# Modulation chunks loaded and summed one merge sooner, and the last norm by column halves, in a two-block float32 model on one core

## The reference, cut to what matters

```python
# first block, for each of the two layers
mod = silu(c) @ ada_w[l] + ada_b[l]                 # 1024 x 3072
shift, scale, gate = split(mod, 3)
h = rms_norm(x, pre_norm[l]) * (1 + scale) + shift
p = split_proj(h @ w_in[l])      # ret, dsa, gla parts and "merge", 3 x 1024 columns
ret, dsa, gl = retention(..), dsa_attention(..), gla(..)   # each normed or gated by silu
g = sigmoid(p["merge"])
y = g0 * (ret @ w_br_ret) + g1 * (dsa @ w_br_dsa) + g2 * (gl @ w_br_gla)
x = x + gate * rms_norm(y @ w_out[l], post_norm[l])
# second block: an even layer (windowed attention and a gated MLP) and an odd one
# (latent attention), with x = x + gate * y, and at the end
out = rms_norm_2(x, final_g)     # x * rsqrt(mean(x*x) + 1e-6) * final_g
```

## Time and profile before

| | us |
|---|---|
| median of three runs | 1077.6 (1077.05 to 1078.86) |
| the profiled execution, its own time | 1079.21 |
| its span | 1077.4 |
| TensorE busy (PE) | 1042.0 |
| TensorE weight loads (PEld) | 757.8 |
| VectorE busy (DVE) | 601.1 |
| ScalarE busy (ACT) | 477.9 |
| GpSimd busy (POOL) | 76.6 |

### The profile page before, as it was taken

One profiled execution on the slowest core, in us unless ns is written; L12 is line 12 of the kernel. 1 busy time (PEld: TensorE's weight loads), 2 busy tenths in 40 slices (PEclk: granted clock), 3 DMA queues, 4 the chain that ended last, 5 costly groups with the idle time before them and its releaser, 6 DMA issues.

```text
span 1077.4 us, 13519 instructions
## 1 busy us (share of the span) xinstructions
PE 1042.0 (97%) x5208; PEld 757.8 (70%) x5208; DVE 601.1 (56%) x1177; ACT 477.9 (44%) x942; POOL 76.6 (7%) x103
## 2 busy tenths in 40 slices
PE   7999999999999999999999999999999999999997
PEld 5688875777467888857874587777677888556553
DVE  2429966595655299754454744236745555245742
ACT  3437547462134365476540353246535423225641
POOL 3001110000000020110000000500000001230000
PEclk9999999999999999999999999999999999999999
DMA  9645432476624355335467362422642015242000
GB/s 385 277 164 203 182 134 101 156 293 276 251 90 170 140 208 203 113 130 219 189 243 304 121 234 79 156 98 79 235 157 103 1 40 220 112 156 98 2 1 39
DMA packets 13743, 171.29 MB, mean 159 GB/s; under 512 B 1504, under 2 KB 1760, under 8 KB 3056
## 3 DMA queue, kind: packets, MB, share of 16 engines
q1 hardware_dynamic: 13216, 168.82, 41.0%
q10 hardware_dynamic: 464, 1.61, 0.4%
HBM read 169.37 MB, written 1.05 MB: 158 GB/s over the span
## 4 chain that ended last, share of the span: by engine, by line
PE 83%; DVE 7%; ACT 6%; DMA 2%; issue 1%; SPq 0%; DVEq 0%; ACTq 0%
PE bank L786 15%; PE bank L1132 8%; PE bank L1081 8%; PE bank L1021 7%; PE bank L1179 6%; PE bank L756 5%; PE bank L1138 5%; PE bank L1114 4%; PE bank L1316 3%; PE bank L764 3%; PE bank L866 3%; PE bank L1393 2%; PE bank L719 2%; PE bank L1381 1%; PE bank L727 1%
## 5 line engine op out<-in xcount | busy, mean ns | idle before, releaser
L1505 ACT ACTIVATE whi<-ring 128x512 fp32r<-128x512 f32 x120 | 73.6, 631 | 65.3 <-PE bank L786 65.3
L2169 DVE TENSOR_TENSOR wlo<-ring,whi 128x512 fp32r<-128x512 f32 x120 | 82.2, 708 | 32.8 <-ACT whi L1505 32.5
L786 PE MATMUL bank<-whi,xhi 128*128 128x512 f32 (+1 forms) x256 | 98.2, 384 | 1.3 <-ACT dsag L1428 1.3
L786 PE MATMUL bank<-wlo,xhi 128*128 128x512 f32 (+1 forms) x256 | 96.4, 377 | 0.0
L786 PE MATMUL bank<-whi,xlo 128*128 128x512 f32 (+1 forms) x256 | 96.4, 376 | 0.0
L764 PE MATMUL bank<-ring,hT 128*128 128x512 f32 (+1 forms) x160 | 61.2, 536 | 0.2 <-ACT hT L1448 0.2
L1138 PE MATMUL bank<-ring,hT 128*128 128x256 f32 (+2 forms) x224 | 57.9, 418 | 3.3 <-ACT hT L1471 2.3
L1021 PE MATMUL bank<-merge_high,xhi 128*128 128x512 f32 x144 | 58.2, 404 | 1.6 <-ACT retqkv L1428 1.1
L1021 PE MATMUL bank<-ring_low,xhi 128*128 128x512 f32 x144 | 56.9, 395 | 0.0
L1021 PE MATMUL bank<-merge_high,xlo 128*128 128x512 f32 x144 | 56.9, 395 | 0.0
L786 PEld LDWEIGHTS bank<-whi,xhi 128*128 128x128 f32 x256 | 48.2, 188 | 11.8 <-ACT dsag L1428 1.6
(11 more groups left out here) (414 smaller groups left out, 2198.3 us busy)
## 6 DMA issues: line engine op xcount, KB each, us to landing
ring<-in_weights SPq DMA_DIRECT2D x73, 2048.0 KB, 8.1
ring<-in_weights SPq DMA_DIRECT2D x5, 1024.0 KB, 5.0
ring<-in_weights SPq DMA_DIRECT2D x2, 1360.0 KB, 10.3
ring<-in_weights SPq DMA_DIRECT2D x1, 1536.0 KB, 8.3
kk<-in_k SPq DMA_DIRECT2D x1, 1120.0 KB, 7.7
X<-in_x SPq DMA_DIRECT2D x1, 1024.0 KB, 14.6
kc<-in_k ACTq DMA_DIRECT2D x1, 1024.0 KB, 10.6
X<-in_context SPq DMA_DIRECT2D x1, 1024.0 KB, 10.1
```

The costliest lines, as they stand in the source:

```text
L786: mm = pe.matmul(o[:, 0:width], a, b[:, q % BUFFERS, at], start=(k == 0 and m == 0), stop=(k == KD - 1 and m == 2))
L1505: act.activation(whi1[:, q % BUFFERS, :], w, ACT.Copy).then_inc(event("hi1_ready"), 1)
L2169: dve.tensor_tensor(wlo1[:, q % BUFFERS, :], piece1(q)[2], whi1[:, q % BUFFERS, :], ALU.subtract).then_inc(event("lo1_ready"), 1)
```

## The change

1. RING1: the chunks ada0 to ada5 are loaded one place sooner, each ahead of merge m + 1, all through slot 0; the merges take slots 2 and 1 in turn.
2. Chunk 0 is summed in g = 6 (layer 0, on VectorE, ahead of gla_take(6)) or behind gla_g (layer 1, on TensorE, in bank 1); chunk m in merge m (VectorE) or behind merge m - 1 (TensorE). Its columns come behind merge m, up to chunk 4; chunk 5's stay where they were. The banks of the sums and columns are new.
3. The last norm goes by column halves: the square, the addition and the product with the gain by halves of 512 columns, the scaling of the low half on VectorE and of the high half on ScalarE, and four stores instead of two.

```diff
-         ("dsa_g", KD * 512, 0), ("gla_g", KD * 512, 1), ("merge0", KD * 512, 2), ("merge1", KD * 512, 0),
-         ("ada0", KD * 512, 1), ("merge2", KD * 512, 2), ("ada1", KD * 512, 1), ("merge3", KD * 512, 0),
-         ("ada2", KD * 512, 1), ("merge4", KD * 512, 2), ("ada3", KD * 512, 1), ("merge5", KD * 512, 0),
-         ("ada4", KD * 512, 1), ("br0", 4 * D, 2), ("ada5", KD * 512, 1), ("br1", 4 * D, 0), ("br2", 4 * D, 1),
+         ("dsa_g", KD * 512, 0), ("gla_g", KD * 512, 1), ("merge0", KD * 512, 2), ("ada0", KD * 512, 0),
+         ("merge1", KD * 512, 1), ("ada1", KD * 512, 0), ("merge2", KD * 512, 2), ("ada2", KD * 512, 0),
+         ("merge3", KD * 512, 1), ("ada3", KD * 512, 0), ("merge4", KD * 512, 2), ("ada4", KD * 512, 0),
+         ("merge5", KD * 512, 1), ("ada5", KD * 512, 0), ("br0", 4 * D, 2), ("br1", 4 * D, 0), ("br2", 4 * D, 1),
...
+        if name == "gla_g1" and summed_on_pe(l, 0):
+            u.append(("s_ada0", 1))
         if name.startswith("merge") and name.endswith("1"):
             m = int(name[5])
-            if summed_on_pe(l, m):
-                u.append((f"s_ada{m}", 0 if m else 1))
-            if m:
-                u.append((f"ada{m - 1}", 1))
+            if summed_on_pe(l, m + 1):
+                u.append((f"s_ada{m + 1}", (0, 0, 4)[m]))
+            if m < MERGES - 1:
+                u.append((f"ada{m}", (1, 1, 5, 2, 1)[m]))
...
+                    if name == "gla_g" and summed_on_pe(l, 0):
+                        ada_rows(u, "ada0", landed("ada0"))
                     if name.startswith("merge"):
                         m = int(name[5])
-                        if summed_on_pe(l, m):
-                            ada_rows(u, f"ada{m}", landed(f"ada{m}"))
-                        if m > 0:
-                            ada1(l, m - 1)
+                        if summed_on_pe(l, m + 1):
+                            ada_rows(u, f"ada{m + 1}", landed(f"ada{m + 1}"))
+                        if m < MERGES - 1:
+                            ada1(l, m)
...
-                    if name.startswith("merge") and summed_on_pe(l, int(name[5])):
-                        m = int(name[5])
+                    if name == "gla_g" and summed_on_pe(l, 0):
+                        ada_out(u, "ada0", msum[0])
+                    if name.startswith("merge") and summed_on_pe(l, int(name[5]) + 1):
+                        m = int(name[5]) + 1
                         ada_out(u, f"ada{m}", msum[m % 2], f"ada{m - 2}" if m > 1 else None)
...
                         if name[0:5] == "merge" and t == 0 and int(name[5]) > 0:
-                            chunk_sum(int(name[5]) - 1)
+                            chunk_sum(int(name[5]))
                         gla_sub(g + 2)
                         gla_mul(g + 1)
+                        if g == 6:
+                            chunk_sum(0)
...
-                        if m == MERGES - 1:
-                            chunk_sum(m)
-                        if m > 0:
-                            own = m - 1 >= SHIFTS
-                            mod_out(u, f"ada{m - 1}", m - 1, l if own else l + 1, conds(l, m - 1))
+                        if m < MERGES - 1:
+                            own = m >= SHIFTS
+                            mod_out(u, f"ada{m}", m, l if own else l + 1, conds(l, m))
...
             for t in range(TT):
-                act.wait_ge(event("x3_ready"), t + 1)
-                act.activation(Y2[:, TT + t, :], X[:, t, :], ACT.Square, accum_out=st2[:, t:t + 1]).then_inc(event("f_ssq"), 1)
-                act.wait_ge(event("f_var"), t + 1)
-                act.activation(st2[:, 8 + t:9 + t], st2[:, 4 + t:5 + t], ACT.Sqrt).then_inc(event("f_std"), 1)
+                for h in range(2):
+                    act.wait_ge(event("x3_ready"), 2 * t + h + 1)
+                    act.activation(Y2[:, TT + t, h * 512:(h + 1) * 512], X[:, t, h * 512:(h + 1) * 512], ACT.Square,
+                                   accum_out=st2[:, 2 * t + h:2 * t + h + 1]).then_inc(event("f_ssq"), 1)
+                act.wait_ge(event("f_part"), t + 1)
+                act.wait_ge(event("f_ssq"), 2 * t + 2)
+                act.activation(st2[:, 8 + t:9 + t], st2[:, 2 * t + 1:2 * t + 2], ACT.Sqrt, scale=1.0 / D,
+                               bias=st2[:, 4 + t:5 + t]).then_inc(event("f_std"), 1)
+                act.wait_ge(event("f_scale"), t + 1)
+                act.activation(Y2[:, t, 512:1024], Y2[:, t, 512:1024], ACT.Copy,
+                               scale=st2[:, 28 + t:29 + t]).then_inc(event("high_out"), 1)
...
+            dve.wait_ge(event("fing_in"), 16)
             for t in range(TT):
-                step(add_half(u, "oout", t, 0, 0, Y2[:, t, 0:512]))
-                add_half(u, "oout", t, 1, 0, Y2[:, t, 512:1024]).then_inc(event("x3_ready"), 1)
-
-                if t == 0:
-                    dve.wait_ge(event("fing_in"), 16)
-                dve.wait_ge(event("f_ssq"), t + 1)
-                dve.tensor_scalar(st2[:, 4 + t:5 + t], st2[:, t:t + 1], 1.0 / D, EPS, ALU.mult, ALU.add).then_inc(event("f_var"), 1)
+                for h in range(2):
+                    c = slice(h * 512, (h + 1) * 512)
+                    add_half(u, "oout", t, h, 0, Y2[:, t, c]).then_inc(event("x3_ready"), 1)
+                    dve.wait_ge(event("x3_ready"), 2 * t + h + 1)
+                    step(dve.tensor_tensor(Y2[:, t, c], X[:, t, c], fing[:, c], ALU.mult))
+                    if h == 0:
+                        dve.wait_ge(event("f_ssq"), 2 * t + 1)
+                        dve.tensor_scalar(st2[:, 4 + t:5 + t], st2[:, 2 * t:2 * t + 1], 1.0 / D, EPS, ALU.mult,
+                                          ALU.add).then_inc(event("f_part"), 1)
+                settle()
                 dve.wait_ge(event("f_std"), t + 1)
-                step(dve.reciprocal(st2[:, 28 + t:29 + t], st2[:, 8 + t:9 + t]))
-                settle()
-                dve.scalar_tensor_tensor(Y2[:, t, :], X[:, t, :], st2[:, 28 + t:29 + t], fing, ALU.mult,
-                                         ALU.mult).then_inc(event("out_ready"), 1)
+                dve.reciprocal(st2[:, 28 + t:29 + t], st2[:, 8 + t:9 + t]).then_inc(event("f_scale"), 1)
+                dve.wait_ge(event("f_scale"), t + 1)
+                dve.tensor_scalar(Y2[:, t, 0:512], Y2[:, t, 0:512], st2[:, 28 + t:29 + t], None, ALU.mult).then_inc(event("low_out"), 1)
```

More of the change, by code:

```diff
@@ L692, in _ @@
             for t in range(TT):
-                sp.wait_ge(event("out_ready"), t + 1)
-                sp.dma_start(out[0, t * P:(t + 1) * P, :], Y2[:, t, :]).then_inc(stored, 16)
-            sp.wait_ge(stored, 16 * TT)
+                for h in range(2):
+                    c = slice(h * 512, (h + 1) * 512)
+                    sp.wait_ge(event(("low_out", "high_out")[h]), t + 1)
+                    sp.dma_start(out[0, t * P:(t + 1) * P, c], Y2[:, t, c]).then_inc(stored, 16)
+            sp.wait_ge(stored, 32 * TT)
         def arrived0(eng, m):
```

## The result

The changed kernel takes 1084.7 us (median of 12 runs, 1083.9 to 1090.9); the kernel before takes 1078.9 us beside it (12 runs, 1077.1 to 1083.0). The ratio is 1.0068, its 95% interval 1.0054 to 1.0081. So the change costs 0.68%, where the prediction had 0.25%, and the time lies 2 us above the range. The ratio is that of the means, 1086.1 over 1078.8; the medians lie 5.8 us apart, 0.54%.

What follows compares the result with a forecast made beforehand. TensorE, busy 97% of the span, was taken as the bound. From 1079.21 us, layer 0 (+3.15 - 1.36 - 1.62 + 1.62), layer 1 (+2.45 - 2.15) and end (-1.05) gave +1.04: forecast 1080.3, range 1077.0 to 1082.6.

Steps and rivals of the forecast that it cites:

- The sign: Whole kernel: slower, forecast 1080.3 us, 0.25% above the old median; forecast chance 0.40.
- the three old waits: Layer 1, TensorE: waits of 0.63, 0.51 and 1.01 us would go, together -2.15 us.
- part 3: Layer 1: earlier sums on TensorE bring a 2.45 us wait ahead of merge 0's second half, less 2.15; net +0.30.
- part 2: Layer 0, new column banks: wait behind merge 3 goes, -1.36, and clock fall, -1.62; merge 4's low part at most 0.3.
- part 4: End of the kernel: the last norm by halves issues the last store 1.05 us sooner, landing time unchanged; -1.05.
- The transfer of merge 2: Layer 0: its load, now behind chunk 0's sum, lands at about 199.3, with 7 us of cover; cost 0.
- Rival (c): Both layers: the new waits don't reach TensorE and only old ones go, 1073.0 us; chance 0.12.
- Part 1: Layer 0: chunk 0's sum ends gla_take(6) 6.0 us later, so TensorE waits 3.15 us at gla_scores(7).
- +1.62: Layer 0: one clock fall behind the new 3.15 us wait, taken to cost 1.62 us.
- rival a: Layer 1: the new 2.45 us wait drops the clock too, +1.62, giving 1081.9 us; chance 0.26.
- +1.04: Whole kernel: sum of all terms on the profiled execution's 1079.21 us, giving 1080.25.
- runs without a profile mostly miss today's fall: Kernel before: median of three runs 1077.6, 1.6 below the profiled one, taken as one clock fall missed.

Runs made afterwards that it cites:

- E10: The changed kernel, with GpSimd's last product KL in layer 0 made to wait for chunk 0's sum; ratio 1.0066 to the kernel before.
- E2: The changed kernel, with chunk 0's sum in layer 0 cut from eight instructions to the first; ratio 1.0002 to the kernel before.
- E7: The changed kernel, with 34 filler matmuls on TensorE ahead of gla_scores(7) in layer 0; ratio 1.0056 to the kernel before.
- E0: The changed kernel run once more, nothing altered; ratio 1.0071 to the kernel before.
- E3: The changed kernel, with the first branch weight br0 loaded ahead of ada5; ratio 1.0063 to the kernel before.
- E5: The changed kernel, with chunk 0's sum in layer 0 spread in pieces over VectorE's idle time; ratio 1.0007 to the kernel before.
- E9: The changed kernel, with 17 filler matmuls on TensorE ahead of gla_scores(7) in layer 0; ratio 1.0027 to the kernel before.
- E8: The kernel before, with the last norm by halves and two new banks, loads and sums unmoved; ratio 0.9993 to the kernel before, 1077.6 us.
- E11: Second run of the changed kernel with layer 0's sum in pieces and layer 1's copy of the sums early; ratio 0.9970 to the kernel before, 1075.3 us.
- E4: The changed kernel, with ScalarE's copy of layer 1's chunk 0 sums ahead of the head roots and Silus; ratio 1.0044 to the kernel before.
- E1: The kernel before, with only the last norm by column halves; ratio 0.9998 to the kernel before.

## Why the prediction was wrong

**Right.** The sign, and the reason for it: two new waits of TensorE, at the places named. Layer 1: 2.4 us ahead of merge 0's second half, predicted 2.45; the three old waits gone, -2.15 (part 3). Merge 4: the wait gone and no low-part cost in its place, 0.3 at another spot (part 2). Last norm: -1.1, predicted -1.05 (part 4), but the agreement is luck: the last store is issued 0.8 us sooner and not 1.05 (ScalarE's half took 0.72 us and not 0.63, the root 0.29 and not 0.20). The other 0.3 come from the issue of the last store to the end of the span, 2.7 us where it was 3.0, which the prediction put at 0. The transfer of merge 2 was hidden, as said. Rival (c), that the waits don't reach TensorE, is out.

**Part 1, the 3.15 us.** The wait was 4.06. The step "6.0 us later" took the durations of the sum from a place where GpSimd was idle. In the new place it was not: +0.88 us on one instruction. The rest of the working holds, as E10 shows with 3.18 us.

**The clock.** Two steps failed by more than that. The first is the price of the fall, "+1.62", read behind a wait of 1.36 us in the earlier trace rows and carried over to a wait twice as long. Direction and place were right; the size was 3.3 to 4.4 us, with 6.8 to 9.2 us of low clock behind the wait in place of 3.4, so 1.7 to 2.8 more than in the sum. The fall after layer 1's wait, left open (rival a), came in half of the eight profiled runs that have this wait (the changed kernel, E2, E7 and E10; not E0, E3, E5 and E9), and cost 1.5 us: from 485.82 to merge 1 at 522.72 it is 36.9 us in the changed kernel, in E0 from 481.18 to 516.55 35.4.

**What was left out.** The second is a term put at nothing, the loads of ada5 and br0. The transfers were followed for merge 2 only, where there were 7 us of cover. The diff reverses br0 and ada5 in SP's order, and so puts br0 behind chunk 4's sum; that costs 1.0 us in each layer in the profiled run, 1.25 and 1.4 in E0, so 2.0 to 2.6 (0.6 to 3.2 in the other kernels with this order).

**The sum again.** On its own terms +1.04; with 0.9, 1.7 to 2.8, 2.0 to 2.6 and 0 to 1.5 it is 5.6 to 8.8 us. The medians differ by 5.8, the means by 7.3. The step from the profiled run to the median of three, that runs without a profile mostly miss today's fall, is not borne out: 12 runs of the kernel before have their median at 1078.9, close to the profiled 1079.2.

**The range.** Its upper end, 1082.6 (its own terms, 1081.9 + 0.3 + 0.25, give 1082.4), was built from rivals that vary one thing, a second fall. No term was there for a longer fall, though the text called the clock the one cost that no row shows.

## What to carry to other kernels

When work is moved ahead of a step that frees a bank, its whole length, less the cover there is, turns into a wait of the engine behind that bank, however idle the moving engine is on average: 6.9 us of sum less some 2.8 us of cover made the 4.06 us here. Put it in pieces into that engine's own waits instead: the same early sum went from 0.7% slower to 0.2 to 0.3% faster, with the copy moved too. A wait that removes itself from the path also removes the cover of the next one, so before a stall is booked as a gain, look for the next operand that is ready with less cover than that. And when the order of loads changes, follow every load that now stands behind another one's release, to the first instruction that reads it.

## What the runs showed of the hardware that was not expected

A low clock is not of one length. It lasted 3.4 us at waits of 1.36 us (before, and at br1 in E3), of 2.08 us (br0 in layer 1, E5), of 2.4 us (layer 1; chunk 4's columns in E8) and of 0.73 and 0.79 us (E10, E11, E9). It lasted 6.8 us in E0, at a wait of 4.05 us, and 10.2 us in four other profiled runs (the changed kernel, E3, E4, E10), at waits of 4.06 and 3.18 us; there it began up to 2.9 us before the wait ended and went on for 7.3 to 9.2 us behind it, though in the changed kernel TensorE was wholly busy with dense 512-column matmuls for the last 5 us of it. Nor does the same wait always bring it: the 1.36 us one dropped the clock in the profiled run before and not in E1, the 2.4 us one in layer 1 in four runs of eight, and in the second block one of 0.73 us did in E10 and E11 (0.50 in the three microseconds behind it); the changed kernel has a wait of that length there too, and kept its clock. What decides on it, and on its length, stays open; no run varied that alone.

An instruction of VectorE with two operands in SBUF, 0.75 us by itself, took 1.635 us beside a GpSimd product of 1.38 us; so it did, to 0.004 us, in each of the profiled runs E0, E3, E4, E7 and E9, which have the two side by side.
